# Weight places, identity, transposed probabilities and keys moved by 64 bytes modulo 128 against their matmul partners

## What is computed

```python
q, k, v, z = jnp.split(h @ w_in, 4, axis=-1)
q = rms_norm(q.reshape(b, s, DA_HEADS, 2, DA_HEAD), q_norm_g) * (DA_HEAD ** -0.5)
k = rms_norm(k.reshape(b, s, DA_HEADS, 2, DA_HEAD), k_norm_g)
...
probs = jax.nn.softmax(scores + bias[None, :, None], axis=-1)
weights = probs[:, :, 0] - lam * probs[:, :, 1]
outs.append(jnp.einsum('bhqk,bkhe->bqhe', weights.astype(v.dtype), vb))
...
o = rms_norm(o, head_norm_g) * (1.0 - lam_0)
o = o.reshape(b, s, BRANCH) * jax.nn.silu(z)
return x + o @ w_out
```

## Time and profile before

| what | value |
|---|---|
| median of 3 runs | 1275.62 us (1274.91 to 1275.89) |
| span of the profiled execution | 1280.3 us |
| instructions | 18355 |
| TensorE matmul busy | 1273.9 us, 7170 matmuls |
| TensorE weight load busy | 1086.2 us |
| VectorE busy | 792.3 us |
| ScalarE busy | 612.0 us |
| GpSimd busy | 298.6 us |
| HBM | 119.72 MB read, 9.44 MB written, 101 GB/s over the span |
| granted TensorE clock | 1.000 |

### The profile page before, as it was taken

How to read it: one execution, slowest core, us unless ns; L and a number is a source line. 1 busy time by engine, 2 the same in 40 slices (tenths; PEclk the granted TensorE clock), 3 DMA queues, 4 the chain that set the end, 5 groups by cost and what they waited for, 6 DMA issues and landing times.

```text
span 1280.3 us, 18355 instructions
## 1 busy us (share of the span) xinstructions
PE 1273.9 (99%) x7170; PEld 1086.2 (85%) x7170; DVE 792.3 (62%) x1578; ACT 612.0 (48%) x1300; POOL 298.6 (23%) x203
## 2 busy tenths in 40 slices
PE   9999999999999999999999999999999999999999
PEld 6788888888899999999888888888888888888787
DVE  5435665443479977877333647676767667677743
ACT  4436654333445444445233445556565555656531
POOL 2023310000055656540001412131312223131110
DMA  6322232233533334243236322222223222223511
GB/s 235 108 58 75 59 99 70 96 98 99 203 127 102 107 122 122 77 133 114 72 110 214 116 66 72 93 74 74 75 74 101 89 75 75 74 76 127 184 59 66
DMA packets 110441, 130.35 MB, mean 102 GB/s; under 512 B 7569, under 2 KB 87697, under 8 KB 110354
## 3 DMA queue, kind: packets, MB, share of 16 engines
q1 hardware_dynamic: 104594, 112.39, 27.3%
q10 hardware_dynamic: 5760, 16.78, 3.6%
HBM read 119.72 MB, written 9.44 MB: 101 GB/s over the span
## 4 chain that ended last, share of the span: by engine, by line
PE 96%; DVE 2%; DMA 0%; issue 0%; ACT 0%; POOL 0%; SPq 0%; DVEq 0%
PE ps L928 17%; PE ps L930 16%; PE ps L929 16%; PE ps L933 7%; PE ps L934 6%; PE ps L935 6%; PE ps L1165 5%; PE ps L1163 5%; PE ps L1166 5%; PE ps L1221 3%; PE ps L1231 1%; PE ps L1203 1%; PE ps L1255 1%; DVE wlo L1610 1%; PE ps L1246 1%; PE ps L1245 1%
## 5 line engine op out<-in xcount | busy, mean ns | idle before, releaser
L1610 DVE TENSOR_TENSOR wlo<-raw,whi 128x512 fp32r<-128x512 f32 (+1 forms) x294 | 232.0, 815 | 188.1 <-ACT whi L1292 187.4
L1292 ACT ACTIVATE whi<-raw 128x512 fp32r<-128x512 f32 (+2 forms) x338 | 208.4, 649 | 116.7 <-PE ps L930 88.3
L928 PE MATMUL ps<-whi,hth 128*128 128x512 f32 x592 | 242.2, 409 | 0.2 <-DVE wlo L1610 0.2
L930 PE MATMUL ps<-wlo,hth 128*128 128x512 f32 x592 | 231.4, 391 | 0.0
L929 PE MATMUL ps<-whi,htl 128*128 128x512 f32 x592 | 231.2, 391 | 0.0
L2044 POOL TENSOR_TENSOR wlo<-raw,whi 128x384 fp32r<-128x384 f32 (+1 forms) x44 | 49.1, 1134 | 415.7 <-ACT whi L1292 415.7
L928 PEld LDWEIGHTS ps<-whi,hth 128*128 128x128 f32 x592 | 111.3, 188 | 26.5 <-issue 5.2
L930 PEld LDWEIGHTS ps<-wlo,hth 128*128 128x128 f32 x592 | 111.2, 188 | 24.5
L929 PEld LDWEIGHTS ps<-whi,htl 128*128 128x128 f32 x592 | 111.6, 189 | 19.1
L933 PE MATMUL ps<-hth,whi 128*128 128x512 f32 (+1 forms) x288 | 111.5, 387 | 0.0
L934 PE MATMUL ps<-htl,whi 128*128 128x512 f32 (+1 forms) x288 | 108.9, 378 | 0.0
(11 more groups left out here) (362 smaller groups left out, 2913.6 us busy)
## 6 DMA issues: line engine op xcount, KB each, us to landing
raw<-in_l_w_in SPq DMA_DIRECT2D x64, 512.0 KB, 4.5
raw<-in_w_gate_up SPq DMA_DIRECT2D x44, 512.0 KB, 4.7
raw<-in_w_in SPq DMA_DIRECT2D x13, 1024.0 KB, 5.1
raw<-in_w_down SPq DMA_DIRECT2D x10, 1024.0 KB, 4.9
raw<-in_l_w_out SPq DMA_DIRECT2D x8, 1024.0 KB, 5.0
raw<-in_w_in SPq DMA_DIRECT2D x26, 256.0 KB, 3.4
raw<-in_w_branch SPq DMA_DIRECT2D x8, 512.0 KB, 3.9
raw<-in_w_out SPq DMA_DIRECT2D x4, 1024.0 KB, 4.9
```

Source lines behind the costliest of these rows:

```text
L928: e.matmul(o, ah, wh[:, cs], start=a, stop=False)
L930: m = e.matmul(o, ah, wl[:, cs], start=False, stop=z)
L1292: return e.activation(out, in_, ACT.Copy, **how)
L1610: return e.tensor_tensor(out, src, hi_part.bitcast(F32), ALU.subtract)
```

## The change

A constant `LINE = 16` (words, 64 bytes) is introduced, and tiles of that size, `gap0`, `gap1` and so on, which nothing reads or writes, are allocated behind `ident`, before `pth` and behind `ptl`, before `pth2` and behind `ptl2`. So every tile behind `ident` starts 64 bytes later, and the probability tiles 64 bytes more. The slots of `whi` and `wlo` begin at 5 x 16 words plus 0 or 2048 in place of 0 or 2048; the places of "gp" stay at 80 words (`SHIFT = 5 * LINE`). `qkh` and `qkl` get 32 words more, and the keys in them begin 16 words behind the end of the queries; `q_or_k` makes the view of one of the two parts, and all that writes or reads them (L1219-1220, L1538, L1927-1930, and the users of `qkh`, `qkl` as places of other operands) is put in its terms. No instruction, wait or DMA is added or left out, and the order stays.

```diff
+LINE = 16
...
+        def gap(stack):
+            return sbuf(stack, f"gap{next(gaps)}", [P, LINE])
+
+        gaps = count()
...
         ident = sbuf(ctx, "ident", [P, P])
+        gap(ctx)
...
-        whi, wlo = ([t[:, 2048 - 2048 * i:4096 - 2048 * i] for i in range(2)] for t in (whi_all, wlo_all))
+        whi, wlo = ([t[:, 5 * LINE + 2048 * (1 - i):5 * LINE + 2048 * (2 - i)] for i in range(2)] for t in (whi_all, wlo_all))
...
+        gap(mix)
         pth_f, pth = both(mix, "pth", [P, CAUSAL])
         ptl_f, ptl = both(mix, "ptl", [P, CAUSAL])
+        gap(mix)
...
-        qkh[0] = sbuf(att, "qkh0", [P, 4, S], F32R)
-        qkl[0] = sbuf(att, "qkl0", [P, 4, S], F32R)
+        qkh[0] = sbuf(att, "qkh0", [P, 4 * S + 2 * LINE], F32R)
+        qkl[0] = sbuf(att, "qkl0", [P, 4 * S + 2 * LINE], F32R)
...
+        gap(att)
         pth2 = sbuf(att, "pth2", [P, CAUSAL], F32R)
         ptl2 = sbuf(att, "ptl2", [P, CAUSAL], F32R)
+        gap(att)
...
+        def q_or_k(t, i):
+            o = (2 * S + LINE) * i
+            return t[:, o:o + 2 * S].rearrange("p (h s) -> p h s", s=S)
...
-                                left = (qkl if i == 2 else qkh)[i2][r, hh, qs]
-                                right = (qkl if i == 1 else qkh)[i2][r, 2 + hh, 0:n]
+                                left = q_or_k((qkl if i == 2 else qkh)[i2], 0)[r, hh, qs]
+                                right = q_or_k((qkl if i == 1 else qkh)[i2], 1)[r, hh, 0:n]
```

More of the change, by code:

```diff
@@ L1 @@
 from contextlib import ExitStack
+from itertools import count
 import concourse.bass as bass
@@ L746, in build @@
         zs = [sbuf(att, f"zs{i}", [P, TB, 256]) for i in range(2)]
-        qkh[1] = sbuf(att, "qkh1", [P, 4, S], F32R)
-        qkl[1] = sbuf(att, "qkl1", [P, 4, S], F32R)
+        qkh[1] = sbuf(att, "qkh1", [P, 4 * S + 2 * LINE], F32R)
+        qkl[1] = sbuf(att, "qkl1", [P, 4 * S + 2 * LINE], F32R)
         xo = [flat(v2h[0][0][:, :, :]), flat(v2l[0][0][:, :, :]), flat(zs[0][:, :, :]), xo3[:, :]]
@@ L762, in build @@
             "ot0": (flat(hth[:, 0:4, :]), flat(htl[:, 0:4, :])), "ot1": (flat(hth[:, 4:8, :]), flat(htl[:, 4:8, :])),
-            "ot2": (flat(qkh[0][:, :, :]), flat(qkl[0][:, :, :])),
+            "ot2": (qkh[0][:, 0:4 * S], qkl[0][:, 0:4 * S]),
         }
@@ L789, in OTH @@
         def OTH(k):
-            return (hth[:, k, :] if k < 8 else qkh[0][:, k - 8, :] if k < 12 else
-                    (x12[0][0][:], x12[0][1][:], qkh[1][:, 0, :], qkh[1][:, 1, :])[k - 12])
+            return (hth[:, k, :] if k < 8 else qkh[0][:, S * (k - 8):S * (k - 7)] if k < 12 else
+                    (x12[0][0][:], x12[0][1][:], qkh[1][:, 0:S], qkh[1][:, S:2 * S])[k - 12])
         def OTL(k):
-            return (htl[:, k, :] if k < 8 else qkl[0][:, k - 8, :] if k < 12 else
-                    (x12[1][0][:], x12[1][1][:], qkl[1][:, 0, :], qkl[1][:, 1, :])[k - 12])
+            return (htl[:, k, :] if k < 8 else qkl[0][:, S * (k - 8):S * (k - 7)] if k < 12 else
+                    (x12[1][0][:], x12[1][1][:], qkl[1][:, 0:S], qkl[1][:, S:2 * S])[k - 12])
         mm, hi, lod, lop = sem("mm"), sem("hi"), sem("lo_dve"), sem("lo_pool")
@@ L851, in build @@
         assert first_slot == 0
-        SHIFT = 80
+        SHIFT = 5 * LINE
         p1_t, sg0_t, u2_t, u3_t, c22_t, c21_t = (tf[0][:, 0:512], tf[0][:, 512:1024], tf[1][:, 0:512],
@@ L1537, in _ @@
                     for i in range(2):
-                        copy(qkh[g % 2][:, 2 * i:2 * i + 2, P * tb:P * tb + P], bv[:, 2 * i:2 * i + 2, :],
+                        copy(q_or_k(qkh[g % 2], i)[:, :, P * tb:P * tb + P], bv[:, 2 * i:2 * i + 2, :],
                              scale=gh[:, 2 + i:3 + i]).then_inc(qk2_hi, 1)
@@ L1926, in _ @@
                     for i in range(2):
-                        at = (slice(0, P), slice(2 * i, 2 * i + 2), slice(P * tb, P * tb + P))
-                        lower_scaled(qkl[g % 2][at], bv[:, 2 * i:2 * i + 2, :], gh[:, 2 + i:3 + i],
-                                     qkh[g % 2][at]).then_inc(qk2_lo, 1)
+                        at = (slice(0, P), slice(0, 2), slice(P * tb, P * tb + P))
+                        lower_scaled(q_or_k(qkl[g % 2], i)[at], bv[:, 2 * i:2 * i + 2, :], gh[:, 2 + i:3 + i],
+                                     q_or_k(qkh[g % 2], i)[at]).then_inc(qk2_lo, 1)
                 elif kind == "vz":
```

## The result

| | us |
|---|---|
| before, median of 6 runs | 1275.74 (1274.57 to 1282.33) |
| after, median of 6 runs | 1285.11 (1284.45 to 1293.35) |
| ratio | 1.0074, 95% interval 1.0045 to 1.0103 |
| profiled execution of before: its time, its span | 1282.33, 1280.3 |
| profiled execution of after: its time, its span | 1293.22, 1291.5 |

The change costs 0.7%, outside the range of the forecast and on its other side. One thing has to be known to read these numbers: in both kernels a single execution can be some 7 to 8 us longer than the others.

A forecast was written before the change was run, and what follows sets the result against it. TensorE's matmul pitch was taken to bound the kernel. Gains of 7.8 (weight places), 2.1 (interruptions) and 1.0 (keys, probabilities), less 1.0 for late results, made 9.9 us: 1275.6 to 1265.7 us, range 1261 to 1276.

The forecast's parts named there:

- The bound: Whole kernel: TensorE is busy practically throughout, so time is the number of matmuls times their start-to-start pitch.
- The formula for windows of settled stretches: TensorE pitch in a window of one kind of matmul: (length of the window + one instruction) / count.
- the first term: Main matmuls outside "gp" with weights in whi and wlo slots: 64 bytes of distance saves 7.8 us.
- the 2.2 ns: Gain per matmul at 64 bytes, read at 256 columns: 117.8 ns in "gp" against 119.7 in other gate/up products.
- The bound that I had set for it from below: Weight places: a gain of 0 at least, if the 2.2 ns belong to 256 columns alone.
- Interruptions: Some 170 groups of transposes, five slower starts behind each: half of 4.3 us taken as gain, 2.1 us.
- Keys, probabilities, identity: Score and probability matmuls in attention gain 1.0 us, between -1 and 2.5; transposes with the identity gain 0.
- Other engines and transfers: VectorE, ScalarE and DMA with tiles moved by 64 bytes: 0, with 0.6 us either way for x's first load.
- The tenth that I gave back to late results: Block ends and score groups: VectorE's results come relatively later once TensorE is faster, costing 1.0 us.
- The second one: Rival: at 512 columns the pitch settles at 232 ns or 235, about +13.7 us, 1289 us; chance 0.12.
- the 5.3 us that it took off: Within the 1289 us rival: 4.3 us already paid behind interruptions and 1.0 us gained, taken off +19 us.
- The first rival: No effect outside "gp": the excess is fixed at 512 columns, time stays 1275.6 us; chance 0.12.

The follow-up runs named there:

- second profiles: The kernels before and after, each unchanged, profiled once more: runs of 1275.23 us (span 1273.5) and 1284.88 us (span 1283.1).
- experiment 7: Kernel before with the slots of whi and wlo at 16 bytes, then at 112 bytes: 1285.56 us, ratio 1.0077, and 1284.32 us, ratio 1.0066.

## Why the prediction was wrong

**The bound held.** TensorE's pitch was the only thing that could move the time, and it did. The formula for windows of settled stretches held too, and the trace has 3,636 matmuls outside "gp" with weights in a slot, near the 3,540 counted.

**The step that failed is the first term**, "3,540 x 2.2 ns = 7.8 us" for the weight places. I took the 2.2 ns from 256 columns and carried them to 512, because the excess over the columns, 13.2 and 13.0 ns, was the same at distance 0. Equal excess at one distance doesn't make it equal at another: at 64 bytes it is 113.4 - 106.7 = 6.7 ns at 256 columns and 229.2 - 213.3 = 15.9 or 233.3 - 213.3 = 20.0 ns at 512. The term measured +11.1 us alone, and at most some 9 us within the change (all stages but "gp" and the start, the other three parts included), in place of -7.8. The bound that I had set for it from below, 0, was false as well; the rows that I had (232 ns passed through behind interruptions, and 235 ns at one of the two places of the forget-gate matmuls) spoke of dearer pitches, and I used them only in the rival.

**The 2.2 ns has two sizes**, since the earlier trace rows came from an execution with "gp" at its dearer level. For the 96 matmuls of 256 columns that the change moves, 2 ns was right (117.5 against 120.0 in the first gate/up block). The usual pitch of "gp" is 113.4, and the gain of 64 bytes there is 118.6 - 113.4 = 5.2 ns. The sign at 256 columns was right, and the run with distance 0 cost 8.1 us. I had remarked that the span was 4.7 us over the median and passed over it. That gap was 6.8 us between the two profiles of the same kernel, and its place was the very stage from which I took the price.

**Interruptions**, forecast -2.1: nothing of it came. The second attention has 111 stretches of 512 columns between interruptions. In each the first distance between starts is long (316 ns, 317 after); the next seven average 230.2 ns in the kernel before and 230.1 after (second profiles), so the excess that I wanted to halve is some 3 ns over seven starts, not 5 over five, and it stayed. What the stage lost, 2.0 us, lies mostly in the 627 distances behind these, 227.0 ns before and 229.0 after.

**Why the loss is 9 us and not 20** (3,540 x 5.7 ns): the two orders pay differently. Where the weights are stationary, 960 matmuls of 512 columns, 64 bytes cost some 6 ns in settled stretches, and the stages that hold them, the first attention and the gates and projections, lost 5.5 us. Where the weights move, 2,580 matmuls, 64 bytes cost some 2 ns in the usual execution (229.2 against 227.1), and 6 only in the down projection of the longer one. All stages behind the projections but "gp" lost some 3.7 us together.

**Keys, probabilities, identity**, forecast -1.0: together with the shift of all tiles they measured +2.1 us (interval 0.9 to 4.2), with no settled pitch altered. In that run's stages the second attention has 0.8 us more than the second profile of before, the last projection 0.6, the start 1.6, of which 1.3 are a longer wait of TensorE for VectorE's `sx` (1.7 us against 0.4). In the changed kernel the dearest score matmuls keep their mean (L1237 with 451 ns, L1221 before). Which of the three parts brings the 1.4 us behind the start wasn't tried alone.

**Other engines and transfers**, forecast 0: right within the profiles, 710 ns before and after for VectorE's subtractions; the one wait that grew, for `xf`, went from 0.5 to 0.6 us (0.8 in the longer execution). The tenth that I gave back to late results had no cause, and nothing became late.

**The rivals.** The second one, "the new distance is the bad one at 512 columns", came true, down to its pitch of 232; it said 1289 and 1285 was measured, because it took 232 ns for every matmul and those with moving weights settle at 229.2 in the usual execution. That it came near is in part luck: its 19 us for the settled pitch are about twice what the stages lost, and the 5.3 us that it took off brought it back. It had a chance of 0.12. The first rival, no effect, and with it the rule of the Trainium skill, page "TensorE: Matmul & The Clock Gate", section "Step-by-step: what each phase is for", that two independent read ports keep a weight load from taking bandwidth from the running matmul, doesn't agree with any of the runs at other distances: by it, as the first rival draws on it, 512 columns would start at one pitch at all of them, and they start at 226.5 to 234.2 ns. That it is a collision of reads is not shown, only that the address of one operand against that of the other, taken modulo 128 bytes and with its sign, moves the pitch, and that at some distances the history of the stream moves it too. That 128 bytes is the period rests on the two runs of experiment 7: in its windows -112 bytes is as good as 16, and 112 as bad as -16.

**What stays open**: why 512 columns settle 32 cycles beyond their length at 0 and 16 bytes and up to 48 elsewhere while 256 have 32 at 0 and 16 at 64; what in a disturbance chooses the level; and why moving weights pay 2 ns for 64 bytes where stationary ones pay 6.

No version that beats the kernel before came out of the runs. Its arrangement, 0 for 512 columns and 64 bytes for most of those of 256, is the best pairing of those measured. What is left are the 96 matmuls of 256 columns in the first gate/up block that have their weights in slots. The change moves them along with the rest, and the row of the block end and first gate/up block has 36.4 us in place of 36.6: 0.2 us, less than can be measured in the time.

## What to carry to other kernels

Where TensorE has no gap left, read the pitch, not the busy time: (window + one instruction) / count over a stretch of like matmuls, in cycles beyond the columns, and take care that the stretch holds nothing else. A placement that helps at one width has to be measured at the other before it is carried there; one run with a single stage moved would have told it here. And when the profiled execution is longer than the timed median, find the stage that holds the difference before taking a price from it.

## What was not expected of the hardware

- One and the same stretch of 1,536 matmuls runs at 117.8 or 113.4 ns a start, 6.8 us in all; the level changes at a wait or a single longer start and holds from there. At 512 columns and 64 bytes there are levels of 229.2 and 233.3 ns.
- The best distance depends on the width: at 256 columns 113.4 or 117.8 ns at 64 bytes against 118.6 to 120 at 0; at 512 columns 226.7 at 0 against 229 to 234.
- The distance has a sign: at 512 columns, in settled stretches, stationary 16 bytes past the moving operand is as good as 0, 16 bytes before it costs 5 to 6 ns, in both orders of weights and tokens.
- Moving one of three passes (`wlo`) by 64 bytes costs no less, 13.4 us, than moving all three, 11.1.
